# Two-layer decoder trunk on one core: the moving operand of most products is read from the last token column to the first

## What is computed

```python
# layer 0
proj = rms_norm(h) @ w_in                      # 2048 -> 6656
h = h + concat(s5(proj_u), retention(proj_q, proj_k, proj_v, proj_g)) @ w_out
# layer 1
c = rms_norm(h) @ w_down                       # 2048 -> 1088
q = rms_norm(cq) @ w_uq;  kv = rms_norm(ckv) @ w_ukv
h = h + attention(q, kv) @ w_out
# after each mixer
a = causal_conv3(rms_norm(h) @ w_up)           # 2048 -> 11264
h = h + (silu(gate) * val) @ w_ffn_down        # 5632 -> 2048
return rms_norm(h, ln_final)
```

## Time and profile before

| | |
|---|---|
| median of two runs | 2203.78 us (2202.25 and 2205.32) |
| profiled execution | 2206.4 us |
| its span, first to last instruction | 2204.5 us |
| PE busy | 2161.4 us, 98% of the span, 18490 matmul records |
| DVE, ACT, POOL busy | 1486.8, 1005.1, 720.8 us |
| mean granted TensorE clock | 0.994 of full speed |
| HBM | 395.3 MB read, 180 GB/s over the span |

### The profile page before, as it was taken

How to read it: one execution, slowest core, us unless ns; L and a number is a source line. 1 busy time by engine, 2 the same in 40 slices (tenths; PEclk the granted TensorE clock), 3 DMA queues, 4 the chain that set the end, 5 groups by cost and what they waited for, 6 DMA issues and landing times.

```text
span 2204.5 us, 47263 instructions
## 1 busy us (share of the span) xinstructions
PE 2161.4 (98%) x18490; PEld 2132.3 (97%) x18490; DVE 1486.8 (67%) x1782; ACT 1005.1 (46%) x1244; POOL 720.8 (33%) x672
## 2 busy tenths in 40 slices
PE   8899999999999999999999999999999999999997
PEld 8889989999999999999999899999999999999997
DVE  6699885777666555666666666677666555666666
ACT  5334335445444444444444455445444444444442
POOL 5699870133434003343211000124434003343311
PEclk9999999999999999999999999999999999999999
DMA  6444444555544565555456433455554565455553
GB/s 265 142 156 158 142 153 172 177 194 187 209 175 178 196 205 208 196 196 191 160 191 214 154 117 129 173 192 192 191 189 180 185 204 214 180 202 191 171 188 117
DMA packets 66137, 398.67 MB, mean 181 GB/s; under 512 B 9216, under 2 KB 11264, under 8 KB 30592
## 3 DMA queue, kind: packets, MB, share of 16 engines
q1 hardware_dynamic: 60192, 391.15, 49.7%
q10 hardware_dynamic: 5856, 6.27, 0.9%
HBM read 395.29 MB, written 2.10 MB: 180 GB/s over the span
## 4 chain that ended last, share of the span: by engine, by line
PE 93%; DVE 4%; DVEq 2%; ACT 1%; issue 1%; DMA 0%; SPq 0%; ACTq 0%
PE PS L1492 27%; PE PS L1493 27%; PE PS L1496 27%; DVE lo L723 1%; PE PS L1487 1%; DVEq L933 1%; PE PS L1489 1%; PE PS L1488 1%; PE PS L1638 1%; PE PS L1590 1%; PE PS L1640 1%; PE PS L1639 1%; PE PS L1604 1%; DVE S L949 1%; PE PS L1842 0%
## 5 line engine op out<-in xcount | busy, mean ns | idle before, releaser
L723 DVE TENSOR_TENSOR lo<-raw,hi 128x1024 fp32r<-128x1024 f32 (+2 forms) x826 | 961.9, 1183 | 513.6 <-ACT hi L363 508.3
L363 ACT ACTIVATE hi<-raw 128x1024 fp32r<-128x1024 f32 (+2 forms) x826 | 787.2, 970 | 791.1 <-PE PS L1496 727.4
L1492 PE MATMUL PS<-XS,hi 128*128 128x256 f32 x3584 | 843.8, 278 | 8.2 <-ACT hi L363 8.2
L1493 PE MATMUL PS<-XS,hi 128*128 128x256 f32 x3584 | 838.5, 277 | 0.0
L1492 PEld LDWEIGHTS PS<-XS,hi 128*128 128x128 f32 x3584 | 674.2, 188 | 11.7 <-issue 10.2
L1493 PEld LDWEIGHTS PS<-XS,hi 128*128 128x128 f32 x3584 | 674.5, 188 | 0.4
L1496 PE MATMUL PS<-XS,lo 128*128 128x256 f32 x3584 | 480.7, 277 | 0.0
L1496 PEld LDWEIGHTS PS<-XS,lo 128*128 128x128 f32 x3584 | 441.1, 188 | 0.0
L1492 PE MATMUL PS<-YF,hi 128*128 128x256 f32 x1408 | 331.8, 276 | 0.0
L1493 PE MATMUL PS<-YF,hi 128*128 128x256 f32 x1408 | 331.8, 276 | 0.0
L1449 POOL TENSOR_TENSOR ctmp<-apad,cws 128x512 f32<-128x512 f32 x88 | 131.9, 1519 | 525.7 <-DVE apad L774 525.7
(11 more groups left out here) (258 smaller groups left out, 2449.9 us busy)
## 6 DMA issues: line engine op xcount, KB each, us to landing
raw<-in_ffn_up SPq DMA_DIRECT2D x176, 1024.0 KB, 4.8
raw<-in_ffn_dn SPq DMA_DIRECT2D x128, 704.0 KB, 4.1
raw<-in_w_in SPq DMA_DIRECT2D x51, 1024.0 KB, 4.8
raw<-in_w_oe SPq DMA_DIRECT2D x16, 1024.0 KB, 4.8
raw<-in_w_oo SPq DMA_DIRECT2D x16, 1024.0 KB, 4.8
raw<-in_mla_dn SPq DMA_DIRECT2D x9, 1024.0 KB, 4.8
raw<-in_w_ukv SPq DMA_DIRECT2D x8, 1024.0 KB, 4.7
raw<-in_w_uq SPq DMA_DIRECT2D x8, 768.0 KB, 4.3
```

The lines of the kernel that those rows point to most:

```text
L363: act.activation(hi[:, p % SLOTS, 0:n], raw[:, u % SLOTS, off:off + n], ACT.Copy).then_inc(hi_ready, 1)
L723: V.tensor_tensor(lo[:, p % SLOTS, 0:n], raw[:, u % SLOTS, off:off + n], f(hi[:, p % SLOTS, 0:n]), ALU.subtract).then_inc(lo_ready, 1)
L1492: mm(PS[:, bank, 0:T], wh, x[:, 0:T], start=first, stop=False)
L1493: mm(PS[:, bank, 0:T], wh, x[:, T:2 * T], start=False, stop=False)
```

## The change

`by_high` and `by_low` get the moving operand and the PSUM output with the token axis reversed. The first column that is read is token 255, and it is written to PSUM column 255; the last is token 0. Each result lands where it did before. The stationary operand, all shapes, all waits, all counts and the order of instructions on every engine stay as they are; `project`, L1638 to L1640, L1826 to L1828 and the plain float32 products keep the forward order.

```diff
             def by_high(bank, wh, x, first):
-                mm(PS[:, bank, 0:T], wh, x[:, 0:T], start=first, stop=False)
-                mm(PS[:, bank, 0:T], wh, x[:, T:2 * T], start=False, stop=False)
+                mm(PS[:, bank, 0:T][:, ::-1], wh, x[:, 0:T][:, ::-1], start=first, stop=False)
+                mm(PS[:, bank, 0:T][:, ::-1], wh, x[:, T:2 * T][:, ::-1], start=False, stop=False)
 
             def by_low(bank, wl, x, last):
-                return mm(PS[:, bank, 0:T], wl, x[:, 0:T], start=False, stop=last)
+                return mm(PS[:, bank, 0:T][:, ::-1], wl, x[:, 0:T][:, ::-1], start=False, stop=last)
```

## The result

The changed kernel takes 2284.65 us in the median of two executions (2272.91 and 2296.39) against 2203.78 us: ratio 1.036, 95% interval 1.032 to 1.040. Five further executions beside nine of the kernel before gave 2269.67 us against 2204.92, ratio 1.030 (1.028 to 1.031). Ratios leave out two executions that lay far above their neighbours, 2420.28 us among these five and 7591.48 us in e5. The 2296.39 us were not seen again in the same kernel, and why that execution was 1% longer than its neighbour is not explained. The change costs 3%. The forecast's centre, 2204 us, was wrong; the time lies inside the stated range of 2190 to 2290 us, near its upper end, only because the range took in the small-cost rival, and that rival is what happened.

The account below looks back on a forecast made before the run. PE was taken to bound the kernel, with 16512 edited products at 113.3 ns. Backward reading and backward PSUM writing were priced at 0 + 0 on the median of 2203.78 us, giving 2204 us, range 2190 to 2290.

Parts of the forecast that it names:

- small-cost rival: Edited products: backward pattern costs some cycles or brings the longer rhythm, 117.3 instead of 113.3 ns, 2270 us; chance 0.12.
- The bound: Whole kernel: PE sets the pace, busy 2161.4 of 2204.5 us; other engines wait for it, and hardly anything hides losses.
- Writing PSUM backward, zero: Output of the edited products: reversed column pairs stay complete, cost zero; the weaker of two zeros, upper bound 216.1 ns.
- Reading backward, zero: Moving operand of the edited products: any address pattern is followed at full pace, cost zero; upper bound 216.1 ns.
- short rhythm: Product stream: the shorter of two paces seen at the same clock, 113.3 ns between starts against 117.3 in the longer.
- nearest in form: Attention's value product, operand in two runs of 128 columns: twelve start 113.6 ns apart, taken as showing zero cost.
- The pace as columns and something on top: Each edited product: 256 columns at one a cycle take 106.7 ns, with some 6.6 ns on top, 113.3 in all.
- The half pace: Edited products: read or write pairs columns only when rising, 216.1 instead of 113.3 ns, 3890 us; chance 0.15.
- near 3751: Matmul count in 560 to 1000 us that would mean the longer rhythm; near 3885 would mean no change.
- The other mark: L1487 to L1489 and L1638 to L1640, which stay forward, keep their pitch while the edited products' moves over 2.7 ns.
- The cover inside the 113.3 ns: Edited products: if the weight load sets the pitch, up to 6.6 ns more column time would not show.

Follow-up runs that it names:

- e5: Against the kernel before: operand read forward, starting four columns late (4 to 259, 252 to 507), other sums; 2274.78 us, ratio 1.031.
- e3: Against the kernel before: only PSUM written backward, moving operand read forward; 2204.74 us, ratio 1.000.
- e11: Against the kernel before: forward, all by_high and by_low products except the first into each PSUM bank stream 240 columns; 2186.24 us, ratio 0.993.
- e4: Against the kernel before: operand read forward, from column 1, and from 255 for the second product, other sums; 2308.94 us, ratio 1.047.
- e12: Against the kernel before: 240 columns except in each bank's first product, read backward, PSUM written forward; 2182.12 us, ratio 0.991.
- e9: Against the kernel before: operand read forward, starting 16 columns late (16 to 271, 240 to 495), other sums; 2284.27 us, ratio 1.037.
- e6: Against the kernel before: groups of four columns taken last to first, forward inside, PSUM in the same order; 2277.89 us, ratio 1.034.
- e10: Against the kernel before: groups of 16 columns taken last to first, forward inside, PSUM in the same order; 2272.09 us, ratio 1.031.
- e8: Against the kernel before: only by_low backward, read and write alike, 5504 of the 16512 products; 2255.03 us, ratio 1.022.
- e2: Against the kernel before: only the moving operand read backward, PSUM written forward; 2271.19 us, ratio 1.030.

## Why the prediction was right or wrong

**The bound.** Right. PE set the pace before and after, its idle time hardly changed (43.1 and 40.6 us), and the loss went into the time nearly one for one: DVE and ACT only wait longer (ACT for PE 793.8 us instead of 727.4 of the earlier trace rows).

**Writing PSUM backward, zero.** Right, by e3 (1.000). I had called it the weaker of the two zeros. The Trainium skill's "PSUM — Partial Sum Buffer" (Specifications), by the letter, spoke of a significant slowdown for a non-contiguous pattern; for a backward run this measurement decides against that reading.

**Reading backward, zero.** This is the step that failed. It costs 4.5 ns (117.8 against 113.3) wherever the stream was in the short rhythm, and nothing where it was in the long one (`YO`). I took zero from the row "nearest in form", twelve products with the moving operand in two runs. That row showed one jump between two long runs, each rising; it said nothing of a run that comes down, nor of another start. Nor was it typical of its own form. The trace of before has 192 of these products, and the other 180 run at 117.7 to 118.0 ns. One group of 24, its first and last:

```profile
1351.33 0.28 PE L1826 MATMUL PS<-hi,CS 128*128 128x256 f32 x1
...
1354.03 0.28 PE L1828 MATMUL PS<-hi,CS 128*128 128x256 f32 x1
```

That is 2.70 us for 23 steps, 117.4 ns by these rounded starts and 117.7 by the exact ones. The forward one-run products around most of these groups are in the longer rhythm too, so this is no proof that a jump costs; but read in full, the form gave no ground for a zero. I should have weighed that equal products ran in two rhythms in the same trace, an effect that I could not explain. A stream whose pace already depends on something unknown is poor ground for a zero.

**The pace as columns and something on top.** I read 113.3 ns as 106.7 ns of columns and 6.6 on top. By e11 that sum doesn't hold: 16 columns fewer save 1.2 ns and not 6.7.

**The half pace.** It did not happen: no pitch came near 216 ns, and the worst read pattern of all these cost 7 ns (e4). Its chance of 0.15 was higher than that of the small cost.

**The small cost.** Its price, 66 us from the two stretches of the earlier trace rows, against 66.4 measured in the span, and its mark, "near 3751" products in 560 to 1000 us, against 3739. That the price agrees so well is partly luck: it took 4.0 ns on all 16512 products, where it was 4.4 to 4.5 ns on about 14900, since some 1650 of them (`YO`, and runs of `XS` mostly in the first 370 us) were in the longer rhythm before the change. It was the right mechanism as far as it went ("throws PE into its longer rhythm"), with a chance of 0.12 that was too low. The other mark held as well: most lines that stay forward kept their time, as these rows of the changed kernel show (busy us, mean ns; L1487 had 47.9 before, L1638 56.3):

```profile
L1638 PE MATMUL PS<-hi,XS 128*128 128x256 f32 x192 | 56.5, 294 | 5.6 <-DVE lo L723 5.6
...
L1487 PE MATMUL PS<-CS,hi 128*128 128x256 f32 x160 | 47.8, 299 | 4.0 <-DVE QRp L1154 4.0
...
L1487 PE MATMUL PS<-XS,hi 128*128 128x256 f32 x16 | 5.3, 334 | 1.9 <-DVE XS L766 1.9
```

The last row is an exception, with 4.5 us and 283 ns before. There the granted clock was at 1.2 GHz for 3.4 us behind a wait of PE for `XS` (0.83 in the mean of 1230 to 1240 us). The run e3 shows the same row at 5.3 us and 333 ns with a ratio of 1.000, so it is no part of the cost of the read.

**The cover inside the 113.3 ns.** I had left open whether up to 6.6 ns of column time could hide there. At 256 columns nothing of the 4.5 ns hid; at 240 all of it did (e11, e12).

**What stays open.** Why the forward run from column 0 or 256 of its row is the only read among those tried at 256 columns that reaches 113.3 ns. It isn't the direction alone (e4, e5, e9), not the order inside 16 or 64 bytes (e6, e10), and not the start on a boundary of up to 64 bytes within the tensor (e5, e9). A boundary beyond 64 bytes, or the distance in SBUF between the moving operand and the weights that are loaded meanwhile, would both fit. The kernel's own declarations speak against the boundary: among the tensors between `XS` and `YF` are some of 156, 2 and 1 floats, so that, unless they are rounded up when they are placed, `YF` lies an odd number of floats behind `XS` and the two can't both start on such a boundary. Yet both are read at 113.3 ns from column 0. The placement isn't recorded, so this is not shown. The kernel has a tensor `gap` of 80 floats between `XS` and the weights that nothing reads; giving it other sizes, forward and backward, would test the second, and was not tried.

## What to carry to other kernels

In a stream of products of 256 columns, each with its own weight load, the address pattern of the moving operand was worth 4 to 7 ns a product here. Only the rising run from column 0 or 256 of its row kept the short pitch, so any other read wants a measurement. Look at the pitch (matmuls in a gapless stretch), since the duration of one product hardly shows it (277 against 282 ns). The order in which PSUM is written was free here. If one trace shows two paces for the same product at the same clock, take the slower one as the first candidate for what a small edit will do, and ask what in the edit could tip it. And before a price is taken from one group of products, look at every group of that form in the trace.

## What the runs showed of the hardware

- The same f32r product of 128 x 128 by 256 columns, at a granted clock of 2.4 GHz, runs at 113.3 ns or near 117.8 ns when read forward from column 0 or 256, and a stretch can be in either rhythm in two kernels that differ only in the order of the PSUM write (665 and 691 products in the same 78 us). A stream stayed in the long one over at least 16 products without a cause of their own (e8), and in the kernel before from 1382.8 to 1476.2 us, until plain float32 products broke it.
- Written to PSUM from the last column to the first, the same products take the same time (ratio 1.000, 0.999 to 1.002, e3).
- Read from the last column to the first they run at 117.8 ns, with the order inside groups of 4 or 16 columns turned back or not (e2, e6, e10).
- A moving operand that starts 1, 4 or 16 columns (for the second product of each pair 255, 252 or 240) from the start of the high part costs 3.1 to 4.7% of the kernel, though it is read forward (e4, e5, e9). In e5 the loads of unchanged weights take 192 ns in the median for the `YF` products of L1492, 188 before.
- 240 columns instead of 256 save 1.2 ns of pitch, not 6.7, and at 240 columns the backward read is free (e11, e12).
